# Gated delta rule: next chunk's gates, masks, key products and first level made beside the present chunk's inverse, which is turned by transposes

## What is computed

```python
gc = jnp.cumsum(g, axis=-1)
...
decay = jnp.exp(jnp.where(incl, gc[..., :, None] - gc[..., None, :], -jnp.inf))
kb = k * beta[..., None]
A = jnp.where(strict, jnp.einsum('nbhid,nbhjd->nbhij', kb, k) * decay, 0.0)
T = A + jnp.eye(C, dtype=F32)
rhs = jnp.concatenate([v * beta[..., None], kb * jnp.exp(gc)[..., None]], axis=-1)
sol = lax.linalg.triangular_solve(T, rhs, left_side=True, lower=True, unit_diagonal=True)
u, w = sol[..., :DV], sol[..., DV:]
qk = jnp.where(incl, jnp.einsum('nbhid,nbhjd->nbhij', q, k) * decay, 0.0)

def step(S, inp):
    q_c, k_c, u_c, w_c, g_c, qk_c = inp
    v_new = u_c - jnp.einsum('bhck,bhkv->bhcv', w_c, S)
    o = jnp.einsum('bhck,bhkv->bhcv', q_c * jnp.exp(g_c)[..., None], S) + jnp.einsum('bhij,bhjv->bhiv', qk_c, v_new)
    g_last = g_c[..., -1:]
    S = S * jnp.exp(g_last)[..., None] + jnp.einsum('bhck,bhcv->bhkv', k_c * jnp.exp(g_last - g_c)[..., None], v_new)
    return S, o
```

## Time and profile before

| what | value |
|---|---|
| time, median of 3 runs | 3452.61 us (3452.24 to 3455.87) |
| the profiled execution, its own time | 3453.79 us |
| its span in the trace | 3452.2 us |
| mean granted clock of TensorE | 0.964 of full |
| TensorE matmul busy | 3248.9 us (94%) |
| vector engine busy | 1945.3 us (56%) |
| ScalarE busy | 1286.9 us (37%) |
| GpSimd busy | 214.3 us (6%) |
| the four chunks, from the first L2294 to the end of the last L2375 | 920.7 to 1173.2 us |

### The profile page before, as it was taken

The page is one execution under the profiler, slowest core; times in us unless marked ns, Lnnn a source line. Parts: engine busy times, 40 slices in busy tenths (PEclk is TensorE's granted clock), DMA queues, the critical chain, the costliest instruction groups (busy, mean ns, idle before and its releaser), DMA issues.

```text
span 3452.2 us, 61433 instructions
## 1 busy us (share of the span) xinstructions
PE 3248.9 (94%) x24682; PEld 3074.8 (89%) x24682; DVE 1945.3 (56%) x2671; ACT 1286.9 (37%) x1832; POOL 214.3 (6%) x254
## 2 busy tenths in 40 slices
PE   7999999998798899998799789999999999999996
PEld 6789999996588899997279679999999999999996
DVE  4544244426766647755412688888888885322224
ACT  5433233326112245433112455555555554321222
POOL 0000000001312000000111000000000000000012
PEclk9999999999799899999999889999999999999997
DMA  7553333322200155676732333333433334432322
GB/s 265 171 177 86 92 92 95 91 64 64 73 1 0 57 185 176 206 234 235 281 128 94 123 105 119 120 117 111 123 116 116 119 120 143 141 108 91 104 92 111
DMA packets 434847, 426.86 MB, mean 124 GB/s; under 512 B 21499, under 2 KB 396556, under 8 KB 426719
## 3 DMA queue, kind: packets, MB, share of 16 engines
q1 hardware_dynamic: 419802, 345.07, 32.6%
q0 software_dynamic: 12352, 69.55, 5.7%
q10 hardware_dynamic: 2576, 10.62, 0.9%
HBM read 391.48 MB, written 33.95 MB: 123 GB/s over the span
## 4 chain that ended last, share of the span: by engine, by line
PE 62%; DVE 6%; DMA 2%; ACT 1%; issue 1%; DVEq 0%; POOL 0%; ACTq 0%; SPq 0%; POOLq 0%
PE ps L2590 14%; PE ps L2419 9%; PE ps L2559 8%; PE ps L2561 8%; PE ps L2560 8%; PE ps L2192 5%; PE ps L2330 2%; PE ps L2514 2%; PE ps L2339 1%; PE ps L2345 1%; DMA cache<-in_cache_mem_k 1%; DVE cache L1889 1%; DMA w_raw<-in_xa_wq 0%; DMA w_raw<-in_w_out 0%; DMA h_in<-h_mid 0%
## 5 line engine op out<-in xcount | busy, mean ns | idle before, releaser
L1428 DVE TENSOR_TENSOR w_low<-w_raw,w_high 128x1024 fp32r<-128x1024 f32 x324 | 396.5, 1225 | 744.3 <-ACT w_high L882 744.0
L2559 PE MATMUL ps<-set_high,w_hi 128*128 128x260 f32 x2464 | 701.5, 285 | 15.0 <-DVE set_low L2004 9.0
L2561 PE MATMUL ps<-set_high,w_lo 128*128 128x260 f32 x2464 | 699.1, 284 | 0.0
L2560 PE MATMUL ps<-set_low,w_hi 128*128 128x260 f32 x2464 | 699.1, 284 | 0.0
L882 ACT ACTIVATE w_high<-w_raw 128x1024 fp32r<-128x1024 f32 x324 | 343.0, 1060 | 708.6 <-PE ps L2192 375.0
L2559 PEld LDWEIGHTS ps<-set_high,w_hi 128*128 128x128 f32 x2464 | 466.9, 190 | 17.6 <-DVE set_low L2004 9.4
L2561 PEld LDWEIGHTS ps<-set_high,w_lo 128*128 128x128 f32 x2464 | 467.9, 190 | 0.0
L2560 PEld LDWEIGHTS ps<-set_low,w_hi 128*128 128x128 f32 x2464 | 466.6, 189 | 1.2 <-issue 1.2
L2192 PE MATMUL ps<-x_high,w_high 128*128 128x260 f32 x2080 | 418.0, 282 | 5.5 <-DVE w_low L1428 4.5
L2192 PE MATMUL ps<-x_low,w_high 128*128 128x260 f32 x2080 | 417.7, 282 | 0.0
L2192 PE MATMUL ps<-x_high,w_low 128*128 128x260 f32 x2080 | 417.0, 282 | 0.0
(11 more groups left out here) (457 smaller groups left out, 5642.3 us busy)
## 6 DMA issues: line engine op xcount, KB each, us to landing
w_raw<-in_w_in SPq DMA_DIRECT2D x96, 512.0 KB
raw<-in_ffn_w_up SPq DMA_DIRECT2D x176, 256.0 KB, 2.9
raw<-in_ffn_w_gate SPq DMA_DIRECT2D x176, 256.0 KB, 3.2
raw<-in_ffn_w_down SPq DMA_DIRECT2D x176, 256.0 KB, 3.0
w_raw<-in_w_out SPq DMA_DIRECT2D x64, 512.0 KB
w_raw<-in_xa_wq SPq DMA_DIRECT2D x64, 512.0 KB
w_raw<-in_xa_wk SPq DMA_DIRECT2D x32, 512.0 KB
w_raw<-in_xa_wv SPq DMA_DIRECT2D x32, 512.0 KB
```

The source lines that it names most:

```text
L1428: dve.tensor_tensor(w_low[:, slot], w_raw[:, (g.slab0 + jj) % RAW], w_high[:, slot].bitcast(F32), ALU.subtract).then_inc(sem("w_low_ready" ...
L2559: pe.matmul(ps[:, bank, 0:HALF], high, set_high[:, kp, x], start=kp == 0, stop=False)
L2560: pe.matmul(ps[:, bank, 0:HALF], high, set_low[:, kp, x], start=False, stop=False)
L2561: ins = pe.matmul(ps[:, bank, 0:HALF], low, set_high[:, kp, x], start=False, stop=kp == KP - 1)
```

## The change

All four chunks are written out, without a loop. The order of each engine's steps is now a list (`in_order`) from which the semaphore counts come.

- The front of chunk n + 1 is placed inside the doubling of chunk n. In each level it stands between the first products of the level and the second: on TensorE the gate sums in level 1, key times key in 2, the turn of the keys in 4, key times query in 5, the turn of the values in 6. On the vector engine: differences in 1, `distance` in 2, `inner` in 3, `qk` in 5. On ScalarE: `grow` in 1, `decay` in 2, the scaled keys in 4, the scaled values in 6. The first level's turn and the start of `inv_t` stand within the state stage, the start of `inv` behind it.
- `inv` isn't made by a product and an addition any more, but is the transpose of `inv_t` (4 TensorE instructions instead of 8), copied out of PSUM by ScalarE instead of added by the vector engine; from level 2 on.
- The front's steps all use the fourth bank of their half. One decay (exponent of minus the distance) serves both masks, where two clipped differences had one exponent each. GpSimd no longer copies keys and values; it makes beta times the lower mask ahead of time. ScalarE scales the keys (twice) and the values by head, 128 x 128 at a time, where the vector engine did it 128 x 512 at a time.
- The tiles that cross a chunk's border exist twice (even, odd).

```diff
+        BESIDE = {"tensor": {1: "grow_ready", 2: "kk_ready", 4: "k_turned", 5: "qk_ready", 6: "v_turned"},
+                  "vector": {1: "differ", 2: "distance", 3: "inner", 5: "qk"},
+                  "scalar": {1: "grow", 2: "decay", 4: "k_rows", 6: "v_rows"}}
...
             pool.wait_ge(*after("normed", 2 * H))
+            for n in range(TT):
+                    pool.tensor_tensor(gate_wide[g][:], per_head(gate, n, g), up, ALU.mult).then_inc(chunk_sem("gate_wide", g), 1)
...
+                    pool.tensor_tensor(inner[n % 2][g][:], per_head(beta, n, g), low, ALU.mult).then_inc(chunk_sem("low_beta", g), 1)
...
+                    pool.wait_ge(*step("decay", g, n))
...
+                    pool.tensor_tensor(inner[n % 2][g][:], inner[n % 2][g][:], decay[g][:], ALU.mult).then_inc(chunk_sem("inner_low", g), 1)
...
+                    pool.tensor_tensor(qk[n % 2][g][:], decay[g][:], up, ALU.mult).then_inc(chunk_sem("qk_mask", g), 1)
...
+                    pool.tensor_tensor(grow[n % 2][g][:], grow[n % 2][g][:], q, ALU.mult).then_inc(chunk_sem("q_scaled", g), 1)
...
+            def by_head(dst, k, scale, n, g):
+                for h in range(HG):
+                    m = n * H + g * HG + h
+                    ins = act.activation(dst[g][:, h], ps[:, k, h * P:(h + 1) * P], ACT.Copy, scale=scale[:, m:m + 1])
+                return ins
...
+            def k_rows(n):
+                for g in range(2):
+                    act.wait_ge(*step("k_turned", g, n))
+                    if n >= 2:
+                        act.wait_ge(*step("S_ready", g, n - 2))
+                    by_head(kbg[n % 2], 4 * g + 3, begc, n, g)
+                    by_head(kdec[n % 2], 4 * g + 3, dgc, n, g).then_inc(chunk_sem("k_rows", g), 1)
...
+                            act.wait_ge(*step(f"inv_ready{l}", g, n))
+                            act.activation(inv[g][:], bank(4 * g + 2), ACT.Copy).then_inc(chunk_sem(f"inv{l}", g), 1)
...
+            def distance(n):
+                for g in range(2):
...
+                    dve.scalar_tensor_tensor(decay[g][:], decay[g][:], -1.0, decay[g][:], ALU.mult, ALU.max).then_inc(chunk_sem("distance", g), 1)
...
+            def solved(n):
+                for l in levels[1:]:
                     for g in range(2):
                         dve.wait_ge(*step(f"half_ready{l}", g, n))
+                        dve.tensor_tensor(half_t[g][:], bank(4 * g), mask[l], ALU.mult).then_inc(chunk_sem(f"half{l}", g), 1)
+                    if n + 1 < TT:
+                        if l == 1:
+                            differ(n + 1)
+                        if l == 2:
+                            distance(n + 1)
+                        if l == 3:
+                            inner_of(n + 1)
+                        if l == 5:
+                            qk_of(n + 1)
                     for g in range(2):
...
                         dve.tensor_tensor(inv_t[g][:], bank(4 * g + 1), inv_t[g][:], ALU.add).then_inc(chunk_sem(f"inv_t{l}", g), 1)
...
+            for n in range(TT):
+                solved(n)
+                if n + 1 < TT:
+                    first_level(n + 1)
+                state(n)
+                if n + 1 < TT:
+                    first_inverse(n + 1)
...
+            def solved(n):
+                for l in levels[1:]:
+                    for g in range(2):
+                        pe.wait_ge(*step(f"inv_t{l - 1}", g, n))
+                        if l == 1 and n:
+                            pe.wait_ge(*step("v_new", g, n - 1))
+                        for h, c in heads(g):
+                            ins = pe.matmul(ps[:, 4 * g, c], inner[n % 2][g][:, h], inv_t[g][:, h], start=True, stop=True)
+                        ins.then_inc(chunk_sem(f"half_ready{l}", g), 1)
+                        if l >= 2:
...
+                            for h, c in heads(g):
+                                ins = pe.transpose(ps[:, 4 * g + 2, c], inv_t[g][:, h], ident[:])
+                            ins.then_inc(chunk_sem(f"inv_ready{l}", g), 1)
+                    if n + 1 < TT:
+                        if l == 1:
+                            grow_of(n + 1)
+                        if l == 2:
+                            kk_of(n + 1)
+                        if l == 4:
+                            k_turn(n + 1)
+                        if l == 5:
+                            qk_of(n + 1)
+                        if l == 6:
+                            v_turn(n + 1)
+                    for g in range(2):
+                        pe.wait_ge(*step(f"half{l}", g, n))
+                        pe.wait_ge(*step(f"inv{l if l >= 2 else 0}", g, n))
...
+                        for h, c in heads(g):
+                            ins = pe.matmul(ps[:, 4 * g + 1, c], inv[g][:, h], half_t[g][:, h], start=True, stop=True)
```

More of the change, by code:

```diff
@@ L209, in more, with tiles @@
             return t
[L211 to L222, removed]
+        def tiles(name):
+            return [more(f"{name}{g}", [P, HG, P]) for g in range(2)]
+        half_t, inv_t, inv = (tiles(n) for n in ("half_t", "inv_t", "inv"))
+        vb, kdec, kbg, grow, inner, qk = ([tiles(f"{n}_even")] for n in ("vb", "kdec", "kbg", "grow", "inner", "qk"))
+        for t, n in ((vb, "vb"), (kdec, "kdec")):
+            t.append(tiles(f"{n}_odd"))
+        S = tiles("S")
         LEVELS = 7
@@ L229, in build @@
         h_rows = more("h_rows", [P, LC * P])
-        rest = XL + CH - top[0]
         assert top[0] <= XL + CH
+        top[0] = M0
+        for t, n in ((kbg, "kbg"), (grow, "grow"), (inner, "inner"), (qk, "qk")):
+            t.append(tiles(f"{n}_odd"))
+        assert top[0] <= M0 + LC * T * 4
+        top[0] = W0 + (RAW + 2 * SPLIT) * SLAB
+        gate_wide, decay = tiles("gate_wide"), tiles("decay")
+        assert top[0] <= nc.sbuf_usable_end
         top[0] = XH
@@ L501, in build @@
         levels = range(LEVELS)
[L502 to L511, removed]
@@ new lines, in first_level, with first_inverse @@
+            def first_level(n):
+                for g in range(2):
+                    dve.wait_ge(*step("half_ready0", g, n))
+                    dve.tensor_tensor(half_t[g][:], bank(4 * g + 3), mask[0], ALU.mult).then_inc(chunk_sem("half0", g), 1)
+                    dve.wait_ge(*step("half0", g, n))
+                    dve.tensor_tensor(inv_t[g][:], half_t[g][:], eye, ALU.add).then_inc(chunk_sem("inv_t0", g), 1)
+            def first_inverse(n):
+                for g in range(2):
+                    dve.wait_ge(*step("inner", g, n))
+                    dve.tensor_tensor(inv[g][:], inner[n % 2][g][:], pairs, ALU.mult).then_inc(chunk_sem("pairs", g), 1)
+                    dve.wait_ge(*step("pairs", g, n))
+                    dve.tensor_tensor(inv[g][:], inv[g][:], eye, ALU.add).then_inc(chunk_sem("inv0", g), 1)
@@ L2354, in chunk, with state @@
+            def state(n):
+                for g in range(2):
+                    pe.wait_ge(*step(f"inv_t{LEVELS - 1}", g, n))
+                    for h, c in heads(g):
+                        ins = pe.matmul(ps[:, 4 * g + 2, c], kbg[n % 2][g][:, h], inv_t[g][:, h], start=True, stop=True)
                     ins.then_inc(chunk_sem("wt_ready", g), 1)
                 for g in range(2):
-                    b = 4 * g
                     pe.wait_ge(*step("wt", g, n))
-                    if later:
-                        pe.wait_ge(*step("S_done", g, n - 1))
@@ L2381, in _ @@
+            k_turn(0)
+            qk_of(0)
+            v_turn(0)
+            first_level(0)
+            for n in range(TT):
+                solved(n)
+                state(n)
             for g in range(2):
```

287 lines of the change are left out of this document (148 added, 139 removed).

## The result

| | before | after |
|---|---|---|
| time, median | 3453.62 us (3452.24 to 3455.87, 4 runs) | 3410.34 us (3409.70 to 3413.31, 4 runs) |
| ratio | | 0.9876, interval 0.9859 to 0.9893 |
| span of the profiled execution | 3452.2 us | 3409.1 us |
| the four chunks, first gate sum to the end of the last state product | 252.65 us | 202.85 us |

The change makes the kernel 43 us (1.2%) faster. In the two profiled executions the phase gave 49.8 us where 47.6 were forecast, and the stages around it took 6.7 us of that back.

A forecast was written before the change was run, and what follows sets the result against it. Nothing outside the engines was taken to bound the four serial chunks, TensorE's issue bounding the doubling. Front 19.5 + 2.4, three chunks of 47.5 and a last of 40.5 make 204.9 us against 252.5: 3405 us, range 3393 to 3428.

The forecast's parts named there:

- A: Likeliest case for the four chunks: levels as summed, 204.9 us against 252.5, 47.6 saved, 3405 us; chance 0.73.
- The overlap and the waits: Covered chunks, priced level by level from the engines' queues: 47.5 us for each of the first three.
- The first gap: TensorE's wait before a chunk's second products of level 1, forecast at about 1.2 us.
- The written-out code: Chunks without a loop: instruction fetching costed at nothing, with 1.5 us a chunk kept for the range.
- The transposes: Twelve half-products a chunk become transposes, 0.44 instead of 0.89 us each: 5.4 us, called a fifth of a chunk's saving.
- ScalarE's scalings: Sixteen key scalings behind level 4: 4.7 us, ending about 0.9 us before they are needed, costed at nothing.
- The front of chunk 0: Uncovered front as one chain: 19.5 us against 16.9, plus 2.4 for its first level at the slow clock.
- The last chunk: Chunk with nothing beside it: 6.6 + 5 x 4.6 + 10.9 = 40.5 us.
- case C: Levels with transposes: TensorE's clock falls to 1.2 GHz, 89 us more minus 47.6, 3494 us; chance 0.06.
- What follows the phase: Output norm, weight loads and output projection behind the chunks: same length expected, so the gain stays.
- B: Ordered queues hold up more: a chunk keeps its 13.3 us of waits, 57.6 each, 3435 us; chance 0.15.
- D: No overlap: a missed wait ties the next front to this chunk's end, 0 to 5 us saved, about 3450; chance 0.03.

The follow-up runs named there:

- Experiment 3: Changed kernel with the next chunk's `pairs` and start of `inv` moved ahead of the state update and first level on the vector engine; 3405.51 us.
- Experiment 4: Experiment 3's kernel with the vector engine's `differ` (level 1) and `inner` (level 3) put behind the additions to `inv_t`; 3401.39 us.
- experiment 1: Changed kernel with `inv` again made by a product and a vector engine addition instead of a transpose, overlap kept; 3420.4 us.
- experiment 2: Changed kernel with each chunk's front put back ahead of its own doubling on all engines, transposes kept; 3440.2 us.
- experiment 6: Changed kernel with eight more 128 x 128 scalings on ScalarE in each front, ahead of the keys' sixteen; 3409.97 us, phase 206.11 us.
- Experiment 5: Kernel before and changed kernel each profiled once more, without edit; spans 3453.7 and 3405.2 us, phases 252.43 and 202.89 us.
- experiment 7: Experiment 4's kernel with the front of chunk 0 spread over all PSUM banks and its `qk` made beside level 1; 3396.62 us.
- experiments 7 and 8: The second of these: experiment 7's kernel with GpSimd's order changed around chunk 0, two later steps held until `inv0` is done; 3394.25 us.

## Why the prediction came out right, and where its sizes were off

The forecast was 3405 us in a range of 3393 to 3428; measured were 3410.34. The likeliest case, A, is what happened. The mechanism is right; that the total came so near is in part luck, since in the phase 3.8 us forecast too many stand against 1.6 too few.

**The overlap and the waits.** The levels were priced one by one, and the middle chunks bear it out: 7.15, 6.3, 5.1, 5.5, 6.3, 5.5 and 11.7 us forecast, 7.03, 6.39, 5.06, 5.48, 6.39, 5.47 and 11.76 measured, 47.5 against 47.58. The first gap was put at about 1.2 us and is 0.97. Experiment 3 shows that it comes from the vector engine's order, as the prediction had it: moved ahead, the start of `inv` takes the gap away. Experiment 4 shows the same for the two smaller ones. The written-out code cost nothing that shows, as taken: the three covered chunks are within 0.06 us of each other. One reading was loose: the wait of 3.51 us for `inner` lies inside the front's first 11.8 us, not behind them.

**The transposes.** The prediction gave them 5.4 us a chunk with the two of the first level, and called that a fifth of the saving. By its own sum a chunk goes from 63.1 to 47.5 us, so it was a third. For the ten of the levels alone the price is 4.5, and experiment 1 measured 3.03, a fifth of the 15.5 us that a chunk really saved. The step that was too large is "product replaced by transpose saves its full difference": it does where nothing stands beside the level (4.7 us in the last chunk), but where steps of the next chunk hold the vector engine up, the shorter instruction in part only makes TensorE wait. The larger part of the gain is the overlap, 31.1 us by experiment 2.

**ScalarE's scalings.** Costed at nothing, with 4.7 us for 16 by the earlier trace rows and 0.9 us of slack. They take 0.25 us each from start to start (1011.28 to 1015.27 for 16), 4.0 in all, and the slack is 1.4. Right, and experiment 6 shows where it ends.

**The front of chunk 0.** Forecast 19.5 us, measured 18.07. The 2.4 us for a slow first level behind it did not occur: the window from 941.80 on has a clock of 1.00. The term was also wrong in kind, since a first level at the slow clock lasted no longer than one at the full clock in experiment 2. These are the two terms that were too large, 3.8 us together.

**The last chunk.** Forecast 40.5, measured 42.11. The prediction's 6.6 us for its level 1 counted the wait for the vector engine at full clock; level 1 lasted 8.09 us. The term left out is the slow clock behind the gap of 2.68 us: the 16 instructions took 3.62 instead of 2.05. The prediction had said against case C that none of its waits is above 1.3 us. Its own 6.6 us hold a longer one: without gate sums beside it, TensorE is done with the first products after 1.8 us and may go on only after 4.75. The phase: 18.07 + 47.52 + 47.58 + 47.57 + 42.11 = 202.85 against 204.9.

**What follows the phase.** "The same length" is right on average over the profiles, within 1 us. In the profiled execution 3.05 us were lost ahead of the phase and 3.65 behind it; that is why a phase that was forecast 2 us too long still went with a time 5 us too short. Experiment 5 shows stretches of unchanged code that vary by as much, and a loss of some 3 us ahead of the phase that may be the change's. The prediction allowed nothing for either.

**The rivals.** B asked for 57.6 us a chunk with gaps over 2 us at the scalings; the chunks are 47.6 and no gap stands there. D asked for a front tied to the end of the chunk, as in experiment 2's kernel; here its pieces stand inside the levels. C asked for the levels to fall to 1.2 GHz. The three covered chunks ran at a granted clock of 1.00, the 2.4 GHz level, with transposes in every level from 2 on. The Trainium skill, "TensorE: Matmul & The Clock Gate", Part 4: PE-mode transpose, says that transposes don't count as busy in the way matmuls do; with 0.88 us of transposes in a level of 5.06 to 6.39, that cost nothing here.

## What to carry to other kernels

A serial chain of small steps beside a stage that keeps one engine busy is worth moving before any of its instructions is made cheaper: the overlap gave 31 us and the cheaper instruction 14, and the cheaper one gave least in the levels where another engine's queue already made TensorE wait. Price such a move level by level, by the queue of each engine, and then look at the two ends that have no neighbour: the uncovered front and the last chunk held 11.3 of the 16.0 us that were found afterwards (by an earlier step on the vector engine, a different order, free banks and GpSimd moved aside). A cost that was hidden can come up when its neighbour gets shorter, as GpSimd's did in experiment 7. Measure the phase as well as the whole: it repeats within 0.2 us, where the rest of this kernel moves by 4 and more.

## What the runs showed that was not expected

**Vector engine and GpSimd.** Operations of 128 x 512 with both inputs in SBUF went from 0.69 to between 1.05 and 1.75 us while GpSimd worked, those that read PSUM stayed at 0.68, and GpSimd slowed from 2.04 to 2.93 us for two (experiments 7 and 8). The single instructions in experiment 7's trace show how: each of the six slow operations ends 0.55 us after the end of the GpSimd instruction that was under way when it began. The longest, for instance, runs from 938.32 to 940.08, and the GpSimd instruction from 937.82 to 939.52. The Trainium skill, "SBUF — State Buffer", SBUF: two separate sides, says that the two engines hold a shared pair of ports in turns, a whole instruction at a time, when the vector engine reads two inputs from SBUF and GpSimd reads there too; by that rule the one waits for the other's instruction to end, and the trace agrees, with 0.55 us after that end for operations that need 0.69 alone. The kernel before had the same in small: in three of its four chunks the first `inv` of L1698 takes 1.09 us beside GpSimd (from 1064.04 in the third) and the second 0.68 to 0.69 without it, which is why has a mean of 837 ns. The prediction priced these operations at 0.69; that GpSimd was done by then in the changed kernel was luck. In the changed kernel itself the `inv` operations at 943.0 to 945.7 fall just behind GpSimd's last mask of that time (until 939.8), and a shorter front brought the two together.

**The clock behind a short gap.** A gap of 2.68 us in the last chunk was followed by 16 instructions in 3.62 us in the changed kernel, and in 3.66 in its second profile. In experiment 1 a gap of 2.69 us was followed by 8 instructions at full clock, and only then by 8 in 1.77 us and 8 in 1.91, which take 1.06 at full clock:

```profile
1100.66 1.16 PE L2453 MATMUL ps<-half_t,inv 128*128 128x128 f32 x8 [2.69 <-DVE half_t L1771]
1101.65 1.77 PE L2459 MATMUL ps<-inv,half_t 128*128 128x128 f32 x8
1103.22 1.91 PE L2453 MATMUL ps<-half_t,inv 128*128 128x128 f32 x8
```

In experiment 6 the same gap was followed by 2.05 us at full clock, and no slow stretch came later in the chunk:

```profile
1094.80 2.05 PE L2466 MATMUL ps<-half_t,inv 128*128 128x128 f32 x16 [2.69 <-DVE half_t L1779]
```

That accounts for the 1.4 us which its last chunk gave back. The gaps of 0.97 us in the covered chunks were never followed by a slow stretch, nor were the three of 2.10 us in experiment 2. So of four executions with a gap of 2.7 us at this place, three lost 1.6 to 1.7 us to the clock and one lost nothing. What decides stays open; with the gap gone (experiments 3, 4, 7 and 8) the last chunk ran without a slow stretch.
